# One attention layer's blocks and the first modulation product, put in another order over three engines

## The reference

```python
cs = silu(c)
mod = cs @ w_ada[i] + b_ada[i]          # 6 parts of 1024: shift, scale, gate, twice
hm = rmsnorm(x, norm_g[i, 0]) * (1 + scale1) + shift1
# layer 1, for each of 8 heads (h) and each block of 128 queries:
sc = q_m @ k_m.T * dh**-0.5 + bias      # m = 0, 1: two maps of 1024 keys, dh = 64
p = softmax(sc)
a = p[0] - lam * p[1]
o = a @ v                               # v has 128 columns
o = rmsnorm(o, subln) * (1 - lam_init)  # then @ w_o
```

## Time and profile before

| | |
|---|---|
| median of 3 runs | 3518.64 us (3512.3, 3518.64, 3518.68) |
| the profiled execution | 3512.4 us, of which its span (first to last instruction) is 3510.5 us |
| TensorE matmuls busy | 3051.6 us, 87% of the span |
| VectorE busy | 1728.5 us, 49% |
| ScalarE busy | 1022.3 us, 29% |
| POOL busy | 441.4 us, 13% |
| granted TensorE clock, mean | 0.911 of full |

### The profile page before, as it was taken

The page is one execution under the profiler, slowest core; times in us unless marked ns, Lnnn a source line. Parts: engine busy times, 40 slices in busy tenths (PEclk is TensorE's granted clock), DMA queues, the critical chain, the costliest instruction groups (busy, mean ns, idle before and its releaser), DMA issues.

```text
span 3510.5 us, 34867 instructions
## 1 busy us (share of the span) xinstructions
PE 3051.6 (87%) x13940; PEld 2464.1 (70%) x13940; DVE 1728.5 (49%) x1898; ACT 1022.3 (29%) x1483; POOL 441.4 (13%) x251
## 2 busy tenths in 40 slices
PE   3698898897678999999967988888687899999996
PEld 2467686673566888888856777767566788888885
DVE  7376872456445333333355655556545533333335
ACT  2222212450223122122124455554432322212212
POOL 3326600227211000000001000000001100000000
PEclk6799999758788999999977999999887899999998
DMA  5463383100210111111102011111121111111111
GB/s 180 157 197 95 104 266 135 38 1 0 108 36 25 48 53 43 48 54 44 51 19 101 19 36 36 42 43 40 55 78 30 30 48 48 48 48 49 51 49 48
DMA packets 262120, 228.22 MB, mean 65 GB/s; under 512 B 6717, under 2 KB 242718, under 8 KB 261982
## 3 DMA queue, kind: packets, MB, share of 16 engines
q1 hardware_dynamic: 250038, 178.27, 16.5%
q0 software_dynamic: 11984, 48.61, 3.7%
HBM read 202.02 MB, written 32.70 MB: 67 GB/s over the span
## 4 chain that ended last, share of the span: by engine, by line
PE 51%; DVE 12%; ACT 7%; issue 5%; POOL 2%; DMA 0%; POOLq 0%; DVEq 0%; ACTq 0%
PE psum_gemm L203 10%; PE psum_gemm L204 9%; PE psum_gemm L207 9%; PE psum_misc L203 5%; PE psum_misc L204 5%; PE psum_misc L207 5%; DVE probs_a L1778 2%; DVE probs_a L1791 2%; DVE probs_b L1778 2%; PE psum_gemm L1562 2%; ACT att_T L1687 1%; DVE mix_out L285 1%; ACT probs_b L1680 1%; DVE x_res L319 1%; ACT probs_a L1680 1%
## 5 line engine op out<-in xcount | busy, mean ns | idle before, releaser
L203 PE MATMUL psum_gemm<-h_hi,w_hi 128*128 128x512 f32 x2128 | 846.7, 398 | 76.9 <-POOL h_lo L346 37.2
L204 PE MATMUL psum_gemm<-h_lo,w_hi 128*128 128x512 f32 x2128 | 838.6, 394 | 0.0
L207 PE MATMUL psum_gemm<-h_hi,w_lo 128*128 128x512 f32 x2128 | 662.7, 393 | 0.0
L203 PEld LDWEIGHTS psum_gemm<-h_hi,w_hi 128*128 128x128 f32 x2128 | 406.5, 191 | 170.5 <-issue 72.3
L204 PEld LDWEIGHTS psum_gemm<-h_lo,w_hi 128*128 128x128 f32 x2128 | 406.1, 191 | 84.3 <-issue 1.0
L207 PEld LDWEIGHTS psum_gemm<-h_hi,w_lo 128*128 128x128 f32 x2128 | 404.6, 190 | 86.1
L1415 ACT ACTIVATE w_hi<-w_raw 128x1024 fp32r<-128x1024 f32 x130 | 137.5, 1058 | 608.4 <-PE psum_misc L207 401.6
L203 PE MATMUL psum_misc<-ffn_act_hi,w_hi 128*128 128x512 f32 x704 | 276.0, 392 | 9.3 <-DVE ffn_act_lo L1460 4.7
L204 PE MATMUL psum_misc<-ffn_act_lo,w_hi 128*128 128x512 f32 x704 | 275.1, 391 | 0.0
L1471 DVE TENSOR_TENSOR mix_out<-mix_out,psum_misc 128x1024 f32<-128x1024 f32 x96 | 117.2, 1221 | 290.6 <-PE psum_misc L207 290.5
L330 POOL TENSOR_TENSOR x_res<-x_res,mix_out 128x1024 f32<-128x1024 f32 x12 | 28.2, 2349 | 1716.0 <-DVE mix_out L285 1716.0
(11 more groups left out here) (283 smaller groups left out, 4851.9 us busy)
## 6 DMA issues: line engine op xcount, KB each, us to landing
w_raw<-in_f_w_up SPq DMA_DIRECT2D x88, 512.0 KB, 3.8
ada_w<-in_w_ada SPq DMA_DIRECT2D x40, 1024.0 KB, 6.7
w_raw<-in_f_w_down SPq DMA_DIRECT2D x44, 512.0 KB, 3.4
w_raw<-in_e_w_in SPq DMA_DIRECT2D x29, 512.0 KB, 4.6
w_raw<-in_o_w_qkv SPq DMA_DIRECT2D x24, 512.0 KB, 3.8
ada_w_first<-in_w_ada SPq DMA_DIRECT2D x4, 2048.0 KB, 16.3
w_raw<-in_e_w_out SPq DMA_DIRECT2D x16, 512.0 KB, 4.0
skew_scratch<-bias_scratch POOLq DMA_DIRECT2D x1, 7680.0 KB, 44.4
```

The lines of the kernel that those rows point to most:

```text
L203: pe.matmul(o, wh, rh[:, k, c], start=(k == 0), stop=False)
L204: pe.matmul(o, wh, rl[:, k, c], start=False, stop=False)
L207: last = pe.matmul(o, wl, rh[:, k, c], start=False, stop=(k == nk - 1))
```

## The change

Setup: the tables of the bias and of lam are loaded before x; lam and the bias rows are computed before x is transposed, and POOL saves the rows before its batches. Batches 0, 1 and 4 of the modulation are made by TensorE directly (`ada_direct_pe`: 16 products with the weights as the stationary operand and one column of c), 2 and 6 by POOL, 3, 5 and 7 by VectorE; batch 3 is placed ahead of `rstd_dve`. POOL's last step of batch 2 waits for the squares to be added, as its buffer lies in the same memory.

Attention: TensorE issues the scores of g+2 first in a turn, ahead of the pieces; ScalarE takes the exponentials of g+2 in turn g, behind `o_part`, and squares the block g-2; VectorE takes `add_bias(g+2)` first in a turn. Scores 1, exponentials 1, additions 1 and combination 0 go ahead of the loop. The deviation of a head moves from the second to the third block of the next (`O_STD`), its transposes and copy from the fourth to the fifth (`O_STEP`).

```diff
@@ -55,7 +55,7 @@
 ADA_START, ADA_XS, ADA_Z, ADA_END = 8, 20, 32, 48
-ADA_POOL = (2, 4, 6)
+ADA_PE, ADA_POOL, ADA_DVE = (0, 1, 4), (2, 6), (3, 5, 7)
 ADA_IN_U = (1, 1, 1, 2, 2, 2, 2, 1)
@@ -396,15 +396,15 @@
...
+            nv, npl = len(ADA_DVE), len(ADA_POOL)
             if b < ADA_START:
...
                     return s_adaP, ADA_POOL.index(b) + 1
-                return s_adaV, b - sum(p < b for p in ADA_POOL) + 1
-            nv = ADA_START - len(ADA_POOL)
+                return s_adaV, ADA_DVE.index(b) + 1
             if b < ADA_XS:
...
             if b < ADA_Z:
-                return s_adaP, len(ADA_POOL) + b - ADA_XS + 1
+                return s_adaP, npl + b - ADA_XS + 1
             return s_adaV, nv + ADA_XS - ADA_START + b - ADA_Z + 1
@@ -441,6 +441,8 @@
...
             pool.wait_ge(s_apc, n + 3)
+            if b == ADA_POOL[0]:
+                pool.wait_ge(s_addV, KT - 1)
             if b >= 2:
@@ -510,14 +512,14 @@
...
             assert n_par == 11
+            sp.dma_start(onehot[:], io["bucket_onehot"]).then_inc(s_atl, 16)
+            sp.dma_start(relt[:], io["rel_table"]).then_inc(s_atl, 16)
+            for n, nm in enumerate(("o_lam_q1", "o_lam_k1", "o_lam_q2", "o_lam_k2")):
+                sp.dma_start(lamv[0:64, n:n + 1], io[nm].rearrange("a (d o) -> (a d) o", o=1)).then_inc(s_atl, 16)
             for n in range(2):
...
                              ).then_inc(s_xin[n], 16)
-            sp.dma_start(onehot[:], io["bucket_onehot"]).then_inc(s_atl, 16)
-            sp.dma_start(relt[:], io["rel_table"]).then_inc(s_atl, 16)
-            for n, nm in enumerate(("o_lam_q1", "o_lam_k1", "o_lam_q2", "o_lam_k2")):
-                sp.dma_start(lamv[0:64, n:n + 1], io[nm].rearrange("a (d o) -> (a d) o", o=1)).then_inc(s_atl, 16)
             for n in range(ADA_START // 2):
@@ -592,11 +594,11 @@
...
                                pattern=[[-1, P]], channel_multiplier=1).then_inc(s_ident, 1)
+            pool.wait_ge(s_fc, 4)
+            pool.dma_start(f_dram, frow[:]).then_inc(s_fs, 16)
             pool.wait_ge(s_cs, 1)
...
                 ada_pool(pool, b)
-            pool.wait_ge(s_fc, 4)
-            pool.dma_start(f_dram, frow[:]).then_inc(s_fs, 16)
             pool.wait_ge(s_small, 1)
@@ -608,48 +610,44 @@
...
             last.then_inc(s_parT, 1)
+            pe.wait_ge(s_lam, 1)
+            pe.matmul(pG[:, 0, 0:2], ones[0:64, :], lamv[0:64, 4:6], start=True, stop=True).then_inc(s_f, 1)
+            pe.wait_ge(s_lexp, 1)
+            pe.wait_ge(s_atl, 96)
+            for n in range(4):
+                pe.matmul(pG[0:8, n // 2, (n % 2) * HALF:(n % 2) * HALF + HALF], relt[:], onehot[:, n * HALF:(n + 1) * HALF],
+                          start=True, stop=True).then_inc(s_f, 1)
             for j in range(KT):
...
                     pe.wait_ge(s_xin[j // 4], 16)
-                if j >= 2:
+                if j < 2:
+                    pe.wait_ge(s_fc, 2 * j + 2)
+                else:
                     pe.wait_ge(s_xC, j - 1)
...
-            pe.wait_ge(s_xC, KT)
-            pe.wait_ge(s_lam, 1)
-            pe.matmul(pG[:, 0, 0:2], ones[0:64, :], lamv[0:64, 4:6], start=True, stop=True).then_inc(s_f, 1)
-            pe.wait_ge(s_lexp, 1)
-            for n in range(4):
-                pe.matmul(pG[0:8, n // 2, (n % 2) * HALF:(n % 2) * HALF + HALF], relt[:], onehot[:, n * HALF:(n + 1) * HALF],
-                          start=True, stop=True).then_inc(s_f, 1)
+            pe.wait_ge(s_cs, 1)
+            for b in (0, 1):
+                ada_direct_pe(pe, b)
             pe.wait_ge(s_addV, KT - 1)
...
             act.activation(cs_c[:], par[:, 0, P_C:P_C + 8], ACT.Silu).then_inc(s_cs, 1)
-            x_squares_act(act, lambda k: act.wait_ge(s_xC, k + 1))
             act.wait_ge(s_f, 1)
             act.activation(nlam[:, 1:3], pG[:, 0, 0:2], ACT.Exp).then_inc(s_lexp, 1)
+            x_squares_act(act, lambda k: act.wait_ge(s_xC, k + 1))
...
                 dve.tensor_copy(par[:, t, 0:PR[t]], pM[:, 0, t * P:t * P + PR[t]]).then_inc(s_parC, 1)
-            for j in range(KT):
-                dve.wait_ge(s_xT, j + 1)
-                dve.tensor_copy(X[:, j], pG[:, j % 2]).then_inc(s_xC, 1)
-                if j == 2:
-                    dve.wait_ge(s_atl, 96)
-                    lv = lamv[0:64, 0:4].rearrange("p (a b) -> p a b", b=2)
-                    dve.tensor_tensor(lamv[0:64, 4:6], lv[:, :, 0], lv[:, :, 1], ALU.mult).then_inc(s_lam, 1)
-            for k in range(1, KT):
-                if k >= 2:
-                    dve.wait_ge(s_addV, k - 1)
-                add_squares(dve, 0, 0, k, s_addV)
+            dve.wait_ge(s_atl, 96)
+            lv = lamv[0:64, 0:4].rearrange("p (a b) -> p a b", b=2)
+            dve.tensor_tensor(lamv[0:64, 4:6], lv[:, :, 0], lv[:, :, 1], ALU.mult).then_inc(s_lam, 1)
             dve.wait_ge(s_lexp, 1)
@@ -660,23 +658,40 @@
...
                                   -1.0, None, ALU.mult).then_inc(s_fc, 1)
+            for j in range(KT):
+                dve.wait_ge(s_xT, j + 1)
+                dve.tensor_copy(X[:, j], pG[:, j % 2]).then_inc(s_xC, 1)
+            for k in range(1, KT):
+                if k >= 2:
+                    dve.wait_ge(s_addV, k - 1)
+                add_squares(dve, 0, 0, k, s_addV)
+            ada_dve(dve, ADA_DVE[0])
+        def ada_direct_pe(pe, b):
+            w = ada_src(pe, b)
+            for m in range(2):
+                for k in range(KT):
+                    last = pe.matmul(pM[:, 1, 512 + 2 * b + m:513 + 2 * b + m], w[:, k, m * P:(m + 1) * P], cs_c[:, k:k + 1],
+                                     start=(k == 0), stop=(k == KT - 1), skip_group_check=True)
+            last.then_inc(s_red, 1)
         def ada_first_pe(pe):
-            for b in range(ADA_START):
-                ada_pe(pe, b)
+            for b in range(2, ADA_START):
+                if b in ADA_PE:
+                    ada_direct_pe(pe, b)
+                else:
+                    ada_pe(pe, b)
...
         def first_mods_dve(dve):
-            dve.wait_ge(s_cs, 1)
-            for b in range(ADA_START):
-                if b == ADA_START - 1:
-                    for u in range(2):
-                        split_lo(dve, u)
-                if b not in ADA_POOL:
-                    ada_dve(dve, b)
+            ada_dve(dve, ADA_DVE[1])
+            for u in range(2):
+                split_lo(dve, u)
+            ada_dve(dve, ADA_DVE[2])
             dve.wait_ge(s_red, ADA_START)
@@ -1523,6 +1538,7 @@
...
         QM = 18
+        O_STD, O_STEP = 2, 4
@@ -1636,20 +1652,23 @@
...
             v_step(0)
+            scores(1)
             for g in range(-1, NB):
-                lo, cut, hi, _ = qkv_range(g)
-                piece(lo, cut)
+                lo, cut, hi, at_end = qkv_range(g)
+                if 0 <= g < NB - 2:
+                    scores(g + 2)
+                if at_end:
+                    piece(lo, cut)
+                    lo = cut
                 if g >= 0:
...
                     step(lambda c: E0[:, g % 3, c * P:(c + 1) * P], s_aT, s_aTl, g + 1)
-                if g + 2 < NB:
-                    scores(g + 2)
                 if g >= 1:
                     av(g - 1)
-                piece(cut, hi)
+                piece(lo, hi)
                 if g >= 0 and g % CH == CH - 1 and g + 1 < NB:
                     v_step((g + 1) // CH)
-                if g >= CH and g % CH == 3:
+                if g >= CH and g % CH == O_STEP:
                     o_step(g // CH - 1)
@@ -1724,9 +1743,8 @@
...
             v_hi(0)
+            probs(1)
             for g in range(-1, NB):
-                if g >= 0 and g + 1 < NB:
-                    probs(g + 1)
                 e = ended(g)
@@ -1734,19 +1752,23 @@
...
                     a_hi(g)
+                if g >= 2:
+                    o_square(g - 2)
                 if g >= 1:
                     o_part(g - 1)
-                    o_square(g - 1)
+                if 0 <= g < NB - 2:
+                    probs(g + 2)
                 if e and e[2]:
...
                     v_hi((g + 1) // CH)
-                if g >= CH and g % CH == 1:
+                if g >= CH and g % CH == O_STD:
                     o_std(g // CH - 1)
-                if g >= CH and g % CH == 3:
+                if g >= CH and g % CH == O_STEP:
                     o_copy(g // CH - 1)
...
                     o_hi(act, g - NB + CH - 1)
+            o_square(NB - 2)
             o_part(NB - 1)
@@ -1820,15 +1842,17 @@
...
             v_lo(0)
+            add_bias(1)
+            combine(0)
             for g in range(-1, NB):
                 e = ended(g)
+                if 0 <= g < NB - 2:
+                    add_bias(g + 2)
                 if e and e[1] < 2:
...
                     a_lo(g)
-                if g + 2 < NB:
-                    add_bias(g + 2)
-                if g + 1 < NB:
+                if 0 <= g < NB - 1:
                     combine(g + 1)
```

## The result

The changed kernel takes 3395.03 us, the median of 4 runs (3388.57 to 3401.04), beside 3518.32 for the kernel before: a ratio of 0.9653, 95% interval 0.9629 to 0.9677, so 123 us less. The prediction said 3397. Its profiled execution is the slowest of its four (3401.04, span 3399.3), and the one of before was the fastest of its own (3512.4, span 3510.5).

A forecast was written before the change was run, and what follows sets the result against it. The prediction took a ScalarE-VectorE ring through the square, stalling TensorE, as the attention's bound. From 3512.4 us it took 101 (attention) and 17 (setup), giving 3394, plus 3 for the runs: 3397, range 3376 to 3436.

The forecast's parts named there:

- The ring: Attention: ScalarE's square awaits VectorE's sum, next exponentials queued behind it; 9.0 to 10.0 us a turn, cut by the change.
- the walk of the prediction: Step-by-step timing of one attention block in the new order on all engines, and of the setup.
- its covers: Attention: slack before results are wanted; some 6 us for exponentials, 3.4 for the combination, 4.7 for bias additions.
- 70.9 + 1.0 + 0.6 = 72.5: Middle head: TensorE's work 70.9, two stalls of 0.5, six projection changeovers of 0.1; 72.5 us against 85.25.
- The stalls of 0.5 behind 18 matmuls: Attention: transposes wait 0.5 us for the combination in blocks with 18 projection matmuls, twice a head.
- The halves' evacuation, the rival on the other side: Rival, chance 0.04: slower, TensorE holds the next projection half for VectorE's low part; 3544 at 3.5 us a place.
- a slide of 0.2: Attention: the next head's first v copy waits for the output's save and slides 0.2 us, with 2 us in hand.
- The prediction's other case: Last seven blocks: at the low clock throughout they take 56 us, a gain of 17, where 50 was taken.
- the 46 that the prediction had named as a sign of being wrong: Setup: adds of squares forecast to end at 41 to 43; ending after 46 would show the prediction wrong.
- its terms, 32 and 14.3: Setup: weights of TensorE's batches 0 and 1 land by 32; both batches, at 7.1 us each, take 14.3.
- The 71 that the prediction gave for batches held by POOL: Setup: by the shared-interface rule VectorE's batches queue with POOL's batch 6, so the scale starts near 71.
- the 3 us put on for the profiled execution: Sum: 3 us added to 3394 because two of three runs before lie 6 us above the profiled one.

The follow-up runs named there:

- e3: The kernel before with only ScalarE's square of an output block taken one block later; 3434.41 us.
- e4: The changed kernel with exponentials of g+1 back at the turn's start and the square of g-1 put back, scores and bias additions still first; 3412.01 us.
- e7: The changed kernel with TensorE's scores of g+2 put back behind the transposes of g; 3502.96 us.
- e5: The changed kernel with only the square of g-1 put back, ahead of the exponentials of g+2; 3501.87 us.
- e6: The changed kernel with only the exponentials of g+1 put back at the start of ScalarE's turn; 3386.07 us.
- e8: The changed kernel with the output's transposes and copy back in the next head's fourth block (O_STEP 3); 3385.55 us.
- e12: The changed kernel run once more, unaltered, on the same chip as e11; 3391.84 us.
- e11: The changed kernel with e6's exponentials, O_STEP 3, e9's POOL wait, and batch 3 moved to TensorE, VectorE's batches 5 and 7 behind rstd; 3383.55 us.
- e1: The kernel before with every attention edit and the old setup; 3414.66 us, ratio 0.9706.
- e2: The kernel before with the setup edits only and the old attention order; 3494.14 us, ratio 0.993.
- e9: The changed kernel with POOL waiting for the adds of squares before the first product of batch 2; 3385.41 us.

## Why the prediction was right

**The ring.** Forecast: the square's wait gone, TensorE the bound. Measured: gone from the list, TensorE 97% busy. e3 shows that the square's place is enough to open the ring: moving it alone brings 10.6 of 12.5 us a head. It isn't the only way. In e4 the square still waits 124.6 us and a head costs only some 2 more than changed, since scores and bias additions first shorten the ring. So the two steps overlap, and neither has a share of its own. e7 and e5 show what the walk of the prediction took for granted: its covers hold only in this order of all three engines. They also show how near the order stands to a loss: either of these two steps put back alone costs over 100 us.

**A head.** Forecast 70.9 + 1.0 + 0.6 = 72.5. Measured 72.6 to 73.3, and 71.3 for the first (71.1 forecast). The spacing inside a head was not as forecast: 8.6 to 9.3 was named as a sign, and combinations are 7.4 to 12.9 apart, in the same pattern in each head. The sum of a head was right, its even pace wasn't. The stalls of 0.5 behind 18 matmuls are there, 12 times in six heads, 7.6/12 = 0.6 each. The halves' evacuation, the rival on the other side, costs 2.5 us of matmul waits and 3.4 of weight loads in six places, all of them v's and all behind the save.

**The save.** Here the walk was wrong and the sum didn't feel it. It had the save landed in 2.9 us and the v copy sliding by 0.2. The save lands 5.4 us after its issue. SP issues a weight load of the same size just ahead of it, at 2027.25 against 2027.47. So it goes in all six heads (5.3 to 5.9), and the seventh save, with no load near, lands in 3.0; 1.5 us behind the load, in e6, it takes 3.3 to 3.5 five times of six. With no load near it isn't always quick either: two of seven before the change took 4.4 and 5.1. The copy of v waits 5.8 us a head. e8 prices it at 0.5 to 0.6 a head, some 3 us in all; the rest was covered. The walk had a slide of 0.2 that costs nothing.

**The last blocks.** Forecast 50, measured 51.1 and 49.2 (e12), with clocks of 0.80 and 0.90. The low level is still there: the row at 2438.63 takes 1.97 and stands behind waits of 1.98 and 0.79, the one at 2431.07 takes 1.09. The prediction's other case had the whole stage at the low level, at 56. Behind it stood the rule of the Trainium skill (TensorE: Matmul & The Clock Gate, HAM oscillation), whose own example has bursts that are shorter than the waits between them. That the clock falls behind waits agrees with the trace, but here TensorE is busy for 39.7 of 51.1 us, and by the mean clock of 0.80, between 0.50 and 1.00, some 60% of the stage ran at the high level. VectorE was to run without gaps at 6.5 to 7.4 a block. It is busy for 43.3 of 51.1 us, stands 5.7 us before ScalarE's copy of earlier outputs, and the blocks are 5.3 to 8.5 apart. So the 50 was near, but the stage isn't the one of the walk. The 4 us that e6 saves here come with the exponentials at the start of the turn: TensorE's busy time falls from 39.7 to 34.9 there, at a clock of 0.93, the same as in e11. Whether the order or the clock comes first in that wasn't taken apart.

**The attention in sum.** 101 forecast, 101.3 in the trace (103.4 in e12), 102 in e1 by medians.

**The setup.** 17 forecast, scale at 66.5. Measured 72.21 in the first trace, and 67.94, 68.67, 70.80, 68.12, 71.16, 67.94 and 67.90 in the seven others that share this setup unchanged (e2, e4 to e8, e12), so 11 to 15.5 gained at the scale. The rows up to the bias rows came as walked: tables issued in 0.34 to 0.60 each, bias rows at 11.46, x transposes at 18.38 (19 forecast), copies done at 31 (30). Three terms were wrong, and two of them cancel.

The adds end at 46.08 where 41 to 43 stood, just past the 46 that the prediction had named as a sign of being wrong (45.4 to 46.0 in the seven others with this setup). The walk let each us that POOL comes later shorten them. POOL's product came 1.0 later in this trace and 2.1 to 2.5 later in six others, and the adds took 15.0 to 15.1 in all of them. Each of POOL's three instructions holds one add for about its own length, whenever it comes (the first add 1 us longer than the product of 3.60 beside it):

```profile
33.46 4.62 DVE L251 TENSOR_TENSOR mix_out<-mix_out 128x1024 f32<-128x1024 f32 x1
37.08 3.21 POOL L440 TENSOR_TENSOR ada_w_first<-ada_w_first 128x1024 f32<-128x1024 f32 x1
38.11 3.25 DVE L251 TENSOR_TENSOR mix_out<-mix_out 128x1024 f32<-128x1024 f32 x1
40.36 2.12 POOL L442 TENSOR_TENSOR ada_w_first<-ada_w_first 128x512 f32<-128x512 f32 x1
41.40 2.17 DVE L251 TENSOR_TENSOR mix_out<-mix_out 128x1024 f32<-128x1024 f32 x1
```

The other four adds take 1.2 each. So a batch of POOL that falls wholly inside the adds cost them 6.2 to 6.4 us in every trace, at starts between 2.4 and 4.8 us behind the first add.

TensorE's batches 0 and 1 were to end at 46.5 (its terms, 32 and 14.3, make 46.3) and so to be what the sums wait for. They started at 29.61, not 32, took 9.43 for the pair and ended at 39.04. The sums waited for the adds instead. That the sums ended near 49.7, for 50.1 by the walk, is the luck of these two errors.

And rstd stands at 56.47 where 50.5 stood (52.84 in e12). VectorE had batch 3 (8.77 and 1.37 beside POOL) ahead of the reciprocal. The walk had that batch on VectorE and didn't put rstd behind it. From rstd to the scale it is 15.7, for 16 forecast (66.5 less 50.5). This term is also what scatters. Batch 3 starts 3 to 4 us ahead of POOL's batch 6, and where one of its steps is still open then (3.7 to 3.8 in place of 0.48), rstd is at 52.8 to 53.1; with two it is at 55.1 and 55.4, with three, as in the first trace, at 56.47. The rest of the 4 us at the scale is batch 4 on TensorE, 4.6 to 4.9 or 7.0. e9 and e11 confirm it: rstd waits for batch 3 in the one and starts at 43.59 in the other, where batch 3 is TensorE's.

Beside these rows stands the rule of the Trainium skill (GPSIMD Engine Reference, Key points), that POOL shares its SBUF interfaces with VectorE's operations with two SBUF inputs. The trace agrees, 15.13 against 8.77 in e9. The 71 that the prediction gave for batches held by POOL lies inside the scales measured (67.9 to 72.2), 66.5 doesn't.

**The batches on TensorE.** Forecast 7.1 each. 6.96 at a clock of 0.50 (1.2 GHz), 4.93 at 0.73 (e12, batch 4), 4.7 each for the first two at 0.75. The forecast's figure is the low level's, as its row (the sums) is.

**The sum.** It came within 2 us of the median, and that closeness is luck. The walk's 118 us between traces measured 111.2 in the first and 122.4 in the second. At the scale the setup gained 1.5 to 6 us less than forecast, by the medians of e2 6 more (23 for 17), and the 3 us put on for the profiled execution are of the same size. The scatter of the changed kernel, 18 us over nine runs, is larger than any of these. What the runs bear out is the attention's part, with its mechanism.

## What to carry to other kernels

Look for a cheap instruction that waits for another engine's last result with work queued behind it that needs nothing from it, and move that one instruction a turn: here one such move gave 85% of the head's gain. Then walk the whole turn on all engines, since an order that fits the other two is worth 12 us a head and a half-restored one can lose it all (e5, e7) or nearly nothing (e4). A wait in the list is not its price: 5.8 us of wait for a save cost 0.5, and 124.6 us of waiting squares in e4 some 2 us a head. When a queue's last wait is removed, look what stands ahead on the engine that takes the result, and not only at when the input is ready.

## What the runs showed of the hardware

VectorE's adds with two inputs in SBUF take 8.77 for seven with POOL idle and 15.0 to 15.1 beside one batch of POOL. A single one takes 1.2 and, beside a POOL instruction, about as long as that one: 3.25 beside 3.21, 2.17 beside 2.12. Scaled additions of 256 columns take 0.48 each with POOL idle and go the same way: 3.85, 2.44 and 1.37 beside POOL's 3.60, 2.40 and 1.32 in the first trace. A save of 512 KB lands in 2.9 to 3.0 us in five of seven heads before the change (4.4 and 5.1 in the two others), in 5.2 to 6.0 when a load of 512 KB is issued 0.2 us before it (after and e12), and in 3.3 to 3.5, but for one, when the load is issued 1.5 us before it. Products with one column in float32 take 0.22 us a record at 1.2 GHz (6.96/32) and 0.15 at a mean clock of 0.73 (4.93/32).
